# Attention block: who makes the low parts of the output weights, and where one ScalarE split stands

## The reference, cut to what matters

```python
def hybrid_layer(x, ...):
    h = rms_norm(x, attn_norm_w)
    proj = h @ w_in
    ret_cols, dsa_cols, dil_cols = jnp.split(proj, ...)
    mixed = jnp.concatenate([retention_mixer(ret_cols, ...),        # 4 heads of 64
                             dsa_mixer(dsa_cols, ...),              # 4 heads, top-64 keys
                             dilated_mixer(dil_cols)], axis=-1)     # 8 heads
    x = x + mixed @ w_out                                           # 1024 x 1024
    h = rms_norm(x, mlp_norm_w)
    return x + jnp.square(jax.nn.relu(h @ w_up)) @ w_down
```

## Time and profile before

| | |
|---|---|
| device time, median of 3 runs | 1204.34 us (1204.0 to 1205.3) |
| profiled execution, its own time | 1207.12 us |
| its span in the trace | 1205.8 us |
| TensorE matmul busy | 1181.9 us, 98% |
| VectorE busy | 812.8 us, 67% |
| ScalarE busy | 688.6 us, 57% |
| GpSimd busy | 279.1 us, 23% |

### The profile page before, as it was taken

How to read it: one execution, slowest core, us unless ns; L and a number is a source line. 1 busy time by engine, 2 the same in 40 slices (tenths; PEclk the granted TensorE clock), 3 DMA queues, 4 the chain that set the end, 5 groups by cost and what they waited for, 6 DMA issues and landing times.

```text
span 1205.8 us, 18861 instructions
## 1 busy us (share of the span) xinstructions
PE 1181.9 (98%) x7688; PEld 1056.1 (88%) x7688; DVE 812.8 (67%) x1044; ACT 688.6 (57%) x956; POOL 279.1 (23%) x181
## 2 busy tenths in 40 slices
PE   8999999999999999999999899999999999999997
PEld 8899999999998888888899688888899977888886
DVE  7888988786576766666888456555556973655554
ACT  6888766666435444445636855544554397554543
POOL 0000000001401201111475522212225663222211
PEclk9999999999999999999999999999999999999999
DMA  9645656545547555553643356565554534565560
GB/s 286 210 140 177 209 179 205 179 141 188 183 151 259 193 196 188 181 199 110 211 141 106 108 166 207 184 209 177 164 185 142 160 119 133 181 227 177 177 206 35
DMA packets 152437, 210.66 MB, mean 175 GB/s; under 512 B 5504, under 2 KB 132640, under 8 KB 151712
## 3 DMA queue, kind: packets, MB, share of 16 engines
q1 hardware_dynamic: 151584, 205.08, 52.3%
q10 hardware_dynamic: 768, 4.39, 1.0%
HBM read 208.37 MB, written 1.08 MB: 174 GB/s over the span
## 4 chain that ended last, share of the span: by engine, by line
PE 78%; ACT 9%; DVE 8%; issue 2%; DMA 1%; SPq 1%; POOL 0%; DVEq 0%; ACTq 0%
PE banks L539 77%; ACT w_hi L1016 3%; ACT tmp L1016 2%; DVE w_lo L1409 2%; PE banks L547 1%; DMA raw<-in_w_in 1%; DVE xbc L1417 1%; ACT probs_dil L1016 1%; ACT L1016 1%; DVE work L1413 1%; DVE lru_u L1417 1%; ACT lru_ab L1016 1%; DVE act L1409 1%; ACT probs_dsa L1016 1%; DVE tmp L1417 0%
## 5 line engine op out<-in xcount | busy, mean ns | idle before, releaser
L539 PE MATMUL banks<-act,w_hi 128*128 128x256 f32 (+1 forms) x2928 | 678.6, 320 | 5.3 <-DVE w_lo L1409 2.3
L539 PEld LDWEIGHTS banks<-act,w_hi 128*128 128x128 f32 x2928 | 479.0, 191 | 52.9 <-issue 8.2
L539 PE MATMUL banks<-act,w_lo 128*128 128x256 f32 x1896 | 521.2, 282 | 0.3 <-DVE w_lo L1409 0.3
L1409 DVE TENSOR_TENSOR w_lo<-raw,w_hi 128x2048 fp32r<-128x2048 f32 (+4 forms) x174 | 376.9, 2167 | 207.1 <-ACT w_hi L1016 206.4
L1016 ACT ACTIVATE w_hi<-raw 128x2048 fp32r<-128x2048 f32 (+1 forms) x191 | 359.6, 1884 | 190.9 <-PE banks L539 185.5
L539 PEld LDWEIGHTS banks<-act,w_lo 128*128 128x128 f32 x1896 | 354.8, 190 | 1.9 <-DVE w_lo L1409 0.5
L539 PE MATMUL banks<-w_hi,act 128*128 128x512 f32 (+1 forms) x1072 | 322.0, 375 | 3.4 <-DVE act L1409 2.8
L539 PEld LDWEIGHTS banks<-w_hi,act 128*128 128x128 f32 x1072 | 196.6, 189 | 42.9 <-issue 7.3
L2013 POOL TENSOR_TENSOR act<-tmp,act 128x512 fp32r<-128x512 f32 x44 | 102.7, 2334 | 440.2 <-ACT act L1016 440.2
L2013 POOL TENSOR_TENSOR w_lo<-raw,w_hi 128x512 fp32r<-128x512 f32 (+1 forms) x120 | 156.0, 1331 | 198.9 <-ACT w_hi L1016 198.9
L539 PE MATMUL banks<-w_lo,act 128*128 128x512 f32 (+1 forms) x536 | 199.4, 372 | 0.0
(11 more groups left out here) (239 smaller groups left out, 827.0 us busy)
## 6 DMA issues: line engine op xcount, KB each, us to landing
raw<-in_w_in SPq DMA_DIRECT2D x64, 1024.0 KB, 5.3
raw<-in_w_up SPq DMA_DIRECT2D x32, 1024.0 KB, 5.4
raw<-in_w_down SPq DMA_DIRECT2D x32, 1024.0 KB, 5.0
raw<-in_w_ffn_in SPq DMA_DIRECT2D x22, 1024.0 KB, 5.1
raw<-in_w_out SPq DMA_DIRECT2D x12, 1024.0 KB, 5.0
raw<-in_w_ffn_out SPq DMA_DIRECT2D x11, 1024.0 KB, 4.9
raw<-in_w_out_ssm SPq DMA_DIRECT2D x8, 1024.0 KB, 5.0
raw<-in_w_out_lru SPq DMA_DIRECT2D x5, 1024.0 KB, 4.9
```

Of the source, the lines that this page charges most:

```text
L539: return mm_ops.matmul(out, lhs, rhs, start=start, stop=stop, skip_group_check=True)
L1409: return ops.tensor_tensor(out, a, b, op)
```

## The change

Two edits. First, GpSimd's share of `out_2` goes from 8 eighths to none: VectorE makes the low parts of all four output tiles of both layers, each in one 128x2048 subtraction in its `lead`. Second, ScalarE's `lead` for the tile out A (it splits the tile two places on, which is out C by this text's count) isn't called at the head of that tile any more, but as a stage "split" behind dil0 step 4, whose ScalarE part is dil0's last copies. The stage is known to ScalarE alone; VectorE's `lead` stays at the head of each tile.

```diff
 POOL_SHARE = {
               "ret_k": 5, "ret_q": 5, "ret_v": 5, "ret_g": 5, "dil_k": 7, "dil_q": 7, "dil_v": 8,
-              "out_2": 8}
+              "out_2": 0}
...
-        put("mid", ("out_2", 4 * l), ("att", l, "dil0", 4), ("att", l, "dsa", 2), ("att", l, "dil1", 1))
+        put("mid", ("out_2", 4 * l), ("att", l, "dil0", 4), ("split", T["out_2", 4 * l]), ("att", l, "dsa", 2), ("att", l, "dil1", 1))
...
-                     "final": final}
+                     "split": lead, "final": final}
+            split_later = [i for (_, i), stages in STAGES.items() if ("split", i) in stages]
...
-            walk(lead, evac, rest, STAGE)
+            walk(lambda i: None if i in split_later else lead(i), evac, rest, STAGE)
```

## The result

The changed kernel takes 1228.81 us (median; 1228.32 to 1229.02) against 1204.82 us before (1204.0 to 1206.11): a ratio of 1.0192, with a 95% interval of 1.0177 to 1.0208. By the medians that is 24.0 us more (by the ratio 23.1). The median of before now has a fourth run in it, 1206.11 us. The two profiled executions are 1228.91 and 1207.12 us, 21.8 us apart.

What follows compares the result with a forecast made beforehand. TensorE, busy 98% of the span, was taken to bound the kernel, with VectorE's and ScalarE's chains setting most of the loss. Layer losses of 8.0 and 9.6 us sum to 17.6, giving a median of 1221.9 us; range 1210 to 1232.

Steps and rivals of the forecast that it cites:

- The walk: Following VectorE, ScalarE and TensorE queues through both edits: 8.0 us lost in first layer, 9.6 in second; chance 0.79.
- VectorE's wait for out A: At the head of dil_q 1, VectorE waits 652.1 to 658.2 for ScalarE's high part, then subtracts to 660.5.
- first stall: In the middle of dil_v 1, TensorE idles 6.1 us for dil0's late probs_t copies.
- The chain from there: After out A's subtraction: retention's step 4, dil0's maxima, exponentials, probs_t copies at 667.05 instead of 660.7.
- bound of +3.6 us: Retention's blocks at 3.5 us instead of 2.6 would add 0.9 each, +3.6 in all.
- Retention without GpSimd: In front of out A: two low parts take about 0.8 us instead of 2.88; TensorE's 1.16 us wait goes.
- The second stall: Behind out A, TensorE waits for a bank, then for copies at 685.7: 3.4 us idle.
- B: Rival: VectorE's wait for out A costs nothing, only gains of 7.3 us remain, 1197.0 us; chance 0.06.
- C: Rival: the stall is paid once, later stalls are hidden behind it, 1209 to 1213 us; chance 0.06.
- D: Rival: clock stays at 1.2 GHz through the out tiles, 8 us more a layer, 1238 us; chance 0.09.
- clock terms: 1.7 us charged behind the first idle; full clock all the way would take 0.6 a layer off.
- The second edit alone: Moved split of out C removes TensorE's 1.64 us idle in both layers and 1.7 us low clock in the first.

Runs made afterwards that it cites:

- move_a: Changed kernel with VectorE's subtraction for out A moved from the head of dil_q 1 to behind retention's step 4 (heads 2, 3): 1215.36 us, ratio 1.0083.
- pool_ab: move_all with the low parts of out A and out B given back to GpSimd: 1203.42 us, ratio 0.9982.
- pool_cd: move_all with the low parts of out C and out D given back to GpSimd: 1199.67 us, ratio 0.9951.
- move_all: Changed kernel with all four of VectorE's subtractions moved behind the attention steps they held back: 1199.37 us, ratio 0.9952.
- fill_both: Changed kernel with unused matmuls added in TensorE's idle time: 25 in dil0 step 3, 9 in dsa step 3: 1224.3 us, ratio 1.0156.
- late_only: Kernel before with only the second edit, ScalarE's later split of out C; GpSimd keeps its share: 1203.41 us, ratio 0.9985.
- vec_only: Kernel before with only the first edit, VectorE making the low parts; split of out C unmoved: 1222.73 us, ratio 1.0145.
- move_all_early: move_all with ScalarE's split of out C back at the head of out A: 1201.09 us, ratio 0.9967.

## Why the prediction was right, point by point

The mechanism was right, the size was too small: I forecast 1221.9 us and the kernel took 1228.81. The walk gave 17.6 us where the profiled executions differ by 21.8, and the reference point took off another 2.7. The range held because it was 10 us wide on either side.

- **VectorE's wait for out A.** Forecast 6.1 us with a subtraction at 658.3; measured 6.18, at 658.00. That it makes the first stall is shown by move_a, where this one subtraction stands elsewhere and the stall is gone.
- **The chain from there.** Forecast maxima at 664.3, `probs_t` copies through at 667.05, TensorE idle 6.1; measured ScalarE at 664.08, value products at 667.03, idle 6.37 (the changed kernel reaches this stretch 0.34 us earlier). Retention's block on this path took 2.65 us, where I took 2.6. My bound of +3.6 us for it was too high: it counted the second block of each layer too, which stands behind dil0's maxima and so not on the path of the first stall.
- **Retention without GpSimd.** The low parts were to take about 0.8 us and take 0.75, and the 1.16 us wait went. The Trainium skill (SBUF — State Buffer, "Who interferes with whom") says that a VectorE instruction with two SBUF inputs contends with a GpSimd instruction that reads SBUF. The traces agree: the low parts take 2.87 us in pool_ab and 0.75 in pool_cd, and the times differ by 3.8 us.
- **The second stall.** Forecast 3.4 us in all; measured 0.80 + 2.74.
- **The rivals.** B fell: TensorE waits in the middle of `dil_v 1`. Of its gain of 7.3 us move_all got 5.8, once the subtractions stood where they hold up nobody. C fell, since the later stalls came. D fell: the clock came back each time. (The 3.4 us in its sum are less than a doubling gives: 3.1 + 2.85 + 0.7 - 1.7 is 4.9, and D would have stood at about 1241.)
- **The mis-sized term: the clock.** I charged 1.7 us behind the first idle and let the second loss fall mainly into waits. Out C started at 700.72, not 698.6, and at 1028.72 in the second layer, not 1024.5. The measured low clock was longer (0.66 over the idle itself, 0.50 for 4 us, 0.73 for 4 more), so the work that followed a 6.4 us idle lost more than the work that followed 1.64 us. And the second loss didn't fall into waits: behind the second idle the slow matmuls stood on the path of dil1's maxima. Until then the first layer was 0.9 us behind the walk (the `tmp` copies ended at 686.6, not 685.7), at these maxima it was 1.9 us behind (692.3, not 690.4), and at out C 2.1. Without low clock fill_both is 0.0156 x 1205 = 19 us slower than before; the walk without its clock terms, against a layer of before without them, gives 8.0 - 0.6 + 1.7 and 9.6 - 0.6, 18.1. The remaining 4.3 us (0.0192 - 0.0156) are the clock, where I had 1.2. The intervals alone leave that figure open by some 3 us either way; the traces of the two kernels give 4.2.
- **The reference point.** I added the 17.6 us, counted from the profiled execution, to the median, which lies 2.8 us lower (2.3 with the fourth run). In the changed kernel the two are the same: 1228.91 profiled, 1228.81 the median. So 2.7 us of the miss are this step, and against the median the kernel loses 2.2 us more than against the profiled execution (24.0 against 21.8). That the profiled execution of before had lost clock in its first layer is shown; that most others had not is the likely reason, from their mean clocks under late_only.
- **The second edit alone** was overrated: 5 us counted, 1.7 measured. In the walk this did no harm, since there both edits were followed together. That it costs about 6 us on top of the first the walk held only in part: it has the split of out C at 677.7 instead of 676.6, 1.1 us a layer, where vec_only and the rows of the changed kernel show 1.95 and a low clock behind it.

## What to carry to other kernels

When work moves to another engine, look first at the place in that engine's queue where it will wait, and for what: here 18 us of VectorE work (8 x 2.29) cost 24 us at one place and, in move_all, went with a gain of 5.8 us at another. Walk the queues from the rows and charge each long idle of TensorE (here 2.7 and 6.4 us) with the slow matmuls behind it. Before you add such a sum to a median, see whether the profiled execution stands at that median. And two edits that are each judged alone may be tied by a wait: a later split is harmless while nobody stands still for it.

## What the runs showed of the hardware

A stretch of 6.4 us without matmuls left TensorE at 1.2 GHz, the lower of its two levels, from 667 to some 673 us (granted clock 0.50 for 4 us, then 0.73 over 4). An idle of 1.64 us did so in the first layer of one execution (0.58 over 4 us) and not in the second (1.00). One of 2.7 us did in the changed kernel (0.68 over 5 us) and in move_a (0.57 over 4), and those of 1.5 us in vec_only and 1.4 us in move_all_early did not (1.00). What decides it in the short cases no run here shows. Added matmuls that compute nothing made a kernel faster (1.0156 against 1.0192), since they stood in idle time. And a subtraction of 128x256 with both inputs in SBUF took 0.37 us on VectorE alone (pool_cd) and 1.44 beside GpSimd's (pool_ab), the mean of two each.
